# A hybrid decoder layer on one core: larger rings for keys and values, attention outputs kept in DRAM, and another order in the merged stage

## What is computed

```python
def _layer(x, S0, past_k, past_v, ...):
    xn = _rms(x, norm1_w)
    zq, zk, zv, hq, hf, hi, hg = _split_proj(xn, w_in)
    q, k, v = _da_qkv(zq, zk, zv, qn_w, kn_w)
    if past_k is None:
        o_da = _da_prompt(q, k, v, lam)          # causal, 1024 tokens
    else:
        o_da = _da_decode(q, k, v, past_k, past_v, lam)   # 2048 cached + 8 new
    o_da = (_rms(o_da, subln_w) * (1.0 - lam_init)).reshape(B, T, DA_WIDTH)
    o_hg, S_new = _hgrn2(hq, hf, hi, hg, lb, S0, hg_norm_w)   # recurrent heads
    h = x + jnp.einsum("btc,cd->btd", jnp.concatenate([o_da, o_hg], axis=-1), w_out)
    y = h + _hier_moe(_rms(h, norm2_w), ...)     # 16 experts, top 1 group, top 2 inside
```

## Time and profile before

| what | us |
|---|---|
| median of 3 runs | 1530.07 |
| lowest and highest of them | 1523.56, 1531.3 |
| the profiled execution | 1530.65 |
| its span, first to last instruction | 1528.9 |
| merged stage, from the barrier before it | 592.3 to 948.2 |
| experts, from about | 1134 |

### The profile page before, as it was taken

The page is one execution under the profiler, slowest core; times in us unless marked ns, Lnnn a source line. Parts: engine busy times, 40 slices in busy tenths (PEclk is TensorE's granted clock), DMA queues, the critical chain, the costliest instruction groups (busy, mean ns, idle before and its releaser), DMA issues. The chain is left out here.

```text
span 1528.9 us, 24713 instructions
## 1 busy us (share of the span) xinstructions
PE 1163.0 (76%) x9100; PEld 874.1 (57%) x9100; DVE 581.6 (38%) x1022; ACT 461.0 (30%) x857; POOL 239.3 (16%) x262
## 2 busy tenths in 40 slices
PE   4699998697979794167666757899839989999940
PEld 3699998486868683055444544677624434444410
DVE  5220110363636363466777773311252111121131
ACT  6111100444444454355555554212100100111121
POOL 4100000000000002121222221212011212222231
PEclk9999999698989897578787779899859999999975
DMA  4420310211111114778788774832133898887567
GB/s 120 110 63 22 84 29 25 74 44 57 57 57 57 57 44 129 231 238 268 245 260 265 244 248 146 302 136 97 62 109 96 230 286 262 253 261 204 128 140 185
DMA packets 160578, 226.50 MB, mean 148 GB/s; under 512 B 16081, under 2 KB 104402, under 8 KB 160402
## 3 DMA queue, kind: packets, MB, share of 16 engines
q1 hardware_dynamic: 133826, 168.63, 33.9%
q0 software_dynamic: 12992, 46.93, 12.3%
q10 hardware_dynamic: 13664, 9.64, 2.2%
HBM read 182.17 MB, written 47.45 MB: 150 GB/s over the span
## 5 line engine op out<-in xcount | busy, mean ns | idle before, releaser
L2135 PE MATMUL ps<-ring,e_xgT 128*128 x400 | 182.1, 609 | 8.7 <-SPq L2056 8.7
L2135 PEld LDWEIGHTS ps<-ring,e_xgT 128*128 128x128 f32 x400 | 76.2, 195 | 97.6 <-issue 97.6
L2164 PE MATMUL ps<-ring,e_hT 128*128 x200 | 92.4, 605 | 16.9 <-ACT e_hT L2193 16.9
L629 PE MATMUL ps<-xh,a_wh 128*128 128x384 f32 (+1 forms) x288 | 101.4, 352 | 0.0
L629 PE MATMUL ps<-xl,a_wh 128*128 128x384 f32 (+1 forms) x288 | 97.3, 338 | 0.0
L629 PE MATMUL ps<-xh,a_wl 128*128 128x384 f32 (+1 forms) x288 | 97.0, 337 | 0.0
L2087 POOL DMA_INDIRECT y_rows<-e_oE,slot_to x32 | 50.5, 1579 | 276.6 <-issue 224.8
L2188 ACT ACTIVATE e_sg<-ps 128x256 f32<-128x256 f32 x32 | 12.3, 383 | 256.2 <-PE ps L2135 243.6
L1559 DVE STREAM_TRANSPOSE d_KT<-d_K 128x2048 f32<-128x2048 f32 x32 | 73.7, 2304 | 23.3 <-DMA d_K<-in_cache_k 23.2
L1087 POOL TENSOR_TENSOR h_X<-h_X,h_q 128x256 f32<-128x256 f32 (+1 forms) x56 | 45.9, 830 | 232.6 <-ACT h_X L1344 117.2
L501 DVE COPY p_vs<-ps 128x256 f32<-128x256 f32 (+1 forms) x36 | 15.3, 424 | 173.5 <-PE ps L449 173.5
(11 more groups left out here) (342 smaller groups left out, 2476.2 us busy)
## 6 DMA issues: line engine op xcount, KB each, us to landing
d_K<-in_cache_k SPq DMA_DIRECT2D x128, 256.0 KB, 3.7
d_V<-in_cache_v SPq DMA_DIRECT2D x128, 256.0 KB, 3.8
ring<-in_w_gate SPq DMA_DIRECT2D x16, 1024.0 KB, 7.8
ring<-in_w_up SPq DMA_DIRECT2D x16, 1024.0 KB, 12.0
ring<-in_w_down SPq DMA_DIRECT2D x16, 1024.0 KB, 13.8
zT<-a_zs POOLq DMA_DIRECT2D x12, 544.0 KB, 3.0
a_w<-in_w_in SPq DMA_DIRECT2D x12, 512.0 KB, 3.8
y_rows<-ring SPq DMA_DIRECT2D x10, 512.0 KB, 2.6
```

The costliest lines, as they stand in the source:

```text
L629: ins = pe.matmul(m.ps[:, 7, 0:w0], left[:, n % 2, k, :], right[:, k, c0:c0 + w0], start=(k == 0 and j == 0), stop=(k == KD - 1 and j == 2))
L2135: ins = pe.matmul(m.ps[:, 2 + u, :], xgT[:, u, k, :], up_k[:, bass.ds(r * KD + k, 1), :].squeeze(1), start=(k == 0), stop=(k == KD - 1))
L2164: ins = pe.matmul(m.ps[:, 6 + b, :], hT[:, u, f * 128:f * 128 + 128], down_w[:, bass.ds(r * FC + f, 1), b * 512:b * 512 + 512].squeeze(1), ...
```

## The change

- **Keys and values.** KR goes from 2 to 3 and VR from 3 to 4, so that the ring of values holds a whole sequence. `load_values` takes the page numbers that `load_keys` read for the same group, and reads none itself.
- **Attention outputs.** `mixT` is split. `mixA` [128, 4, 1088] holds the attention half only until the prompt attention ends; GpSimd stores it, head by head, to a DRAM tensor `mix_rows`, and waits at the end of that block for all four stores. `mixH` is the recurrent half, `mixS` the attention output of the 64 new tokens. Mix loads `mix_rows` back in two DMAs (512 KB and 1.5 MB) on ScalarE's queue, and `split_mix` rounds and subtracts each half by its own instruction: four per tile instead of two.
- **VectorE.** `maximum` comes right after `picked_out`, ahead of `cumulate`, `with_keys` and `subs` 1. `subs` 5 and 6 of a unit are done at the start of that unit, after `collect`, and no longer at the end of the one before.
- **ScalarE.** `maps` comes ahead of `decays`, `load_next` and `norm`. `level_exps` 5 and 6 of a unit stand after `turned_keys`, ahead of `gates` of the next.
- **TensorE.** `output` comes after two groups of `values`, not three.

```diff
@@ -113,19 +113,22 @@
-        m.mixT = sb("mixT", [128, KD, TOK])
+        m.mixH = sb("mixH", [128, HEADS, TOK])
+        m.mixS = sb("mixS", [128, HEADS, NS])
+        m.mix_rows = nc.dram_tensor("mix_rows", (HEADS, 128, SEQ), F32, kind="Internal").ap()
         m.hn_rows = nc.dram_tensor("hn_rows", (TOK, D), F32, kind="Internal").ap()
...
-        m.z_stored, m.v_stored = (ctx.enter_context(nc.semaphore(n)) for n in ("z_stored", "v_stored"))
+        m.z_stored, m.v_stored, m.mix_stored = (ctx.enter_context(nc.semaphore(n)) for n in ("z_stored", "v_stored", "mix_stored"))
         with ExitStack() as middle:
...
                 m.xh = early.enter_context(nc.sbuf_tensor("xh", [128, KD, TOK], F32R))
+                m.mixA = early.enter_context(nc.sbuf_tensor("mixA", [128, HEADS, TOK], F32))
                 m.halves = early.enter_context(nc.sbuf_tensor("halves", [128, 128], F32))
@@ -468,7 +471,7 @@
                 for g, (c0, w0) in enumerate(GROUPS):
-                    dst = m.mixT[:, bass.ds(t + HEADS * n, 1), c0:c0 + w0].squeeze(1)
+                    dst = (m.mixA, m.mixH)[n][:, bass.ds(t, 1), c0:c0 + w0].squeeze(1)
                     ins = act.activation(dst, m.ps[:, 3 * n + g, 0:w0], ACT.Copy)
@@ -593,6 +596,9 @@
                     pool.sem_inc(z_left, 1)
+                pool.wait_ge(head_done, h + 1 + 1)
+                pool.dma_start(m.mix_rows[h, :, :], m.mixA[:, h, 0:SEQ]).then_inc(m.mix_stored, 16)
+            pool.wait_ge(m.mix_stored, HEADS * 16)
@@ -683,7 +689,7 @@
                 for n, s in enumerate((sq, sk)):
-                    z = m.mixT[:, bass.ds(h + HEADS * n, 1), :].squeeze(1)
+                    z = (m.mixA, m.mixH)[n][:, bass.ds(h, 1), :].squeeze(1)
                     act.activation(s[:, :], z, ACT.Square).then_inc(squared[n], 1)
@@ -759,7 +765,7 @@
             def prepare(h):
-                zq, zk = (m.mixT[:, bass.ds(h + HEADS * n, 1), :].squeeze(1) for n in range(2))
+                zq, zk = (mix[:, bass.ds(h, 1), :].squeeze(1) for mix in (m.mixA, m.mixH))
                 dve.wait_ge(r_ready[0], h + 1)
@@ -806,7 +812,7 @@
                 dve.wait_ge(ro_ready, h + 1)
-                dve.scalar_tensor_tensor(m.mixT[:, h, 0:SEQ], oT[:, :], m.subw[:, :], ro[:, :],
+                dve.scalar_tensor_tensor(m.mixA[:, h, 0:SEQ], oT[:, :], m.subw[:, :], ro[:, :],
                                          ALU.mult, ALU.mult).then_inc(head_done, 1)
@@ -832,7 +838,7 @@
     KEYS = PAGES * PAGE
-    KR, VR = 2, 3
+    KR, VR = 3, 4
     assert UNITS == DB
@@ -947,7 +953,7 @@
         def gate_of(n):
-            return m.mixT[:, n // 2 + HEADS, n % 2 * W:n % 2 * W + wide(n)]
+            return m.mixH[:, n // 2, n % 2 * W:n % 2 * W + wide(n)]
@@ -987,6 +993,8 @@
+            pages_of = {}
+
             def page_numbers(g):
@@ -994,14 +1002,14 @@
             def load_keys(g):
-                pages = page_numbers(g)
+                pages = pages_of[g] = page_numbers(g)
                 if g >= KR:
...
             def load_values(g):
-                pages = page_numbers(g)
+                pages = pages_of.pop(g)
                 if g >= VR:
@@ -1271,9 +1279,10 @@
                     sample_states(n)
-                for g in range(3):
-                    values(n, g)
+                values(n, 0)
+                values(n, 1)
                 output(n)
+                values(n, 2)
                 values(n, 3)
@@ -1426,19 +1435,21 @@
             logs(0)
             decays(0)
             load_next(1)
-            level_exps(0, 1, LEVELS)
+            level_exps(0, 1, 5)
             for n in range(UNITS):
                 more = n + 1 < UNITS
                 turned_keys(n)
+                level_exps(n, 5, LEVELS)
                 if more:
                     gates(n + 1)
                     logs(n + 1)
+                maps(n)
+                if more:
                     decays(n + 1)
                     if n + 2 < UNITS:
                         load_next(n + 2)
                 if n:
                     norm(n - 1)
-                maps(n)
                 if more:
                     level_exps(n + 1, 1, 2)
                 new_map_out(n)
@@ -1448,7 +1459,7 @@
                 if more:
-                    level_exps(n + 1, 2, LEVELS)
+                    level_exps(n + 1, 2, 5)
                 squares(n)
@@ -1619,43 +1630,45 @@
                 more = n + 1 < UNITS
                 if n:
                     collect(n - 1)
+                    subs(n, 5)
+                    subs(n, 6)
                 for i in range(3):
                     take(n, i)
                 if more:
                     queries(n + 1)
                 if n:
                     picked_out(n - 1)
+                maximum(n)
                 if more:
                     cumulate(n + 1)
                     with_keys(n + 1)
-                    subs(n + 1, 1)
-                maximum(n)
                 for i in range(3, 6):
                     take(n, i)
+                if more:
+                    subs(n + 1, 1)
                 states(n)
                 if more:
                     keys(n + 1, 0)
                 sums(n)
+                if more:
+                    subs(n + 1, 2)
                 if n:
                     finish(n - 1)
                 if more:
-                    subs(n + 1, 2)
                     keys(n + 1, 1)
                     subs(n + 1, 3)
                 if n % 2:
                     sample_states(n)
                 if more:
+                    keys(n + 1, 2)
                     subs(n + 1, 4)
-                    keys(n + 1, 2)
-                    subs(n + 1, 5)
-                    subs(n + 1, 6)
                     keys(n + 1, 3)
             collect(UNITS - 1)
             picked_out(UNITS - 1)
             finish(UNITS - 1)
             dve.wait_ge(d_ready, 1)
             ro = P[:, HEADS * NS:2 * HEADS * NS].rearrange("p (h t) -> p h t", h=HEADS)
-            dve.scalar_tensor_tensor(m.mixT[:, 0:HEADS, SEQ:TOK], m.kS[:, :, :], m.subw[:, :], ro, ALU.mult, ALU.mult)
+            dve.scalar_tensor_tensor(m.mixS[:, :, :], m.kS[:, :, :], m.subw[:, :], ro, ALU.mult, ALU.mult)
 def mix_phase(nc, a, m):
@@ -1705,6 +1718,7 @@
         gate = sem("m_gate")
+        mixA, mix_in = sb("m_mixA", [128, HEADS, SEQ]), [sem("m_mix_in0"), sem("m_mix_in1")]
         w_rounded, w_split, mix_rounded, mix_split = (sem(f"m_{n}") for n in (
@@ -1776,9 +1790,15 @@
                     pool.sem_inc(gate, 1)
-                pool.tensor_copy(mh[:, u, :, 0:n], m.mixT[:, :, cols(t)]).then_inc(mix_rounded, 1)
-                pool.wait_ge(mix_rounded, t + 1)
-                pool.tensor_tensor(ml[:, u, :, 0:n], m.mixT[:, :, cols(t)], mh[:, u, :, 0:n], ALU.subtract).then_inc(mix_split, 1)
+                o, g = mixA[:, :, cols(t)] if t < NT else m.mixS[:, :, :], m.mixH[:, :, cols(t)]
+                ho, hg = mh[:, u, 0:HEADS, 0:n], mh[:, u, HEADS:KD, 0:n]
+                pool.tensor_copy(hg, g).then_inc(mix_rounded, 1)
+                if t in (0, 2):
+                    pool.wait_ge(mix_in[t // 2], 16)
+                pool.tensor_copy(ho, o).then_inc(mix_rounded, 1)
+                pool.wait_ge(mix_rounded, 2 * t + 2)
+                pool.tensor_tensor(ml[:, u, HEADS:KD, 0:n], g, hg, ALU.subtract).then_inc(mix_split, 1)
+                pool.tensor_tensor(ml[:, u, 0:HEADS, 0:n], o, ho, ALU.subtract).then_inc(mix_split, 1)
             split_mix(0)
@@ -1812,7 +1832,7 @@
                     if b == 0:
-                        pe.wait_ge(mix_split, t + 1)
+                        pe.wait_ge(mix_split, 2 * t + 2)
                     if t >= 2:
@@ -1869,6 +1889,8 @@
         def _(act):
+            for i, c in enumerate((slice(0, 256), slice(256, SEQ))):
+                act.dma_start(mixA[:, :, c], m.mix_rows[:, :, c].rearrange("h p n -> p h n")).then_inc(mix_in[i], 16)
             load_ln_exp(nc, act)
```

## The result

The changed kernel takes 1516.98 us (median of four runs, 1514.59 to 1520.32), the kernel before 1529.25 (1523.56 to 1531.3): a ratio of 0.992, with a 95% interval of 0.9893 to 0.9947. It is faster, by 12 us. I had forecast 1504 in a range of 1485 to 1523: the sign and the range hold, the size doesn't. Less than half of the 26 us that I counted came. So the traces show some 16 us between the kernels where the medians show 12.

What follows compares the result with a forecast made beforehand. A chain of waits, not a full engine, was taken to set the merged stage's pace. Terms 3.6 - 16.4 - 18.6 + 0 + 4.5 = -26.9 against 1530.65 gave 1503.7, said as 1504; range 1485 to 1523.

Steps and rivals of the forecast that it cites:

- the term of the odd units: Merged stage, units 1, 3 and 5: 36.5 us each from the last key transpose to TensorE's end of the unit.
- D to D: Between ends of the last key transpose for units 1 and 7: six units, three pairs of 73.5, 220.5 us.
- C: Rival: transfers are the bound, pairs stay at 79.7 us, total 1522, or 1525 with mix's upper end; chance 0.09.
- D: Rival, slower: the last key group is late in every unit of the merged stage, 1539 and above; chance 0.07.
- E: Rival: the wait for values stays, their last group still late; pairs gain 4, total 1518; chance 0.03.
- Edge of the attention, +3.6: End of the prompt attention: GpSimd's last store and its wait add 3.6 us; ends 3.0 and 5.
- Unit 0, -16.4: First unit of the merged stage: key groups sent earlier save 16.4 us; ends -15 and -19.5.
- Even units, 37.0: Merged stage, units 2, 4 and 6: 37.0 us from TensorE's start, ScalarE held 4.0 by its DMA issues.
- rival A: More hidden than counted: even units 4.0 shorter, odd ones 1 shorter, 15 less in all, 1489; chance 0.20.
- Unit 7: Last unit of the merged stage, 33.3 us before: change 0, with 2 to 3 us each way.
- Start of mix: Mix reads 2 MB more: +4.5 us, ends 1 and 7; 6.9 if all of it delays the output weights.
- B: Rival: half of the pairs' gain, keys late and `norm` dearer; pairs give 9, mix 7, total 1516; chance 0.16.

Runs made afterwards that it cites:

- the fastest kernel: The changed kernel with sample states early, DMA issues on GpSimd, norm and squares first, and TensorE's order undone: 1476.91 us, 0.9635 of before.

## Why the prediction was right, and where it was wrong

The forecast gain was 26 us and 12 came. The step that failed is the term of the odd units, 36.5 us each: they took 39.9, 42.9 and 38.3, which is 11.6 of the 13.8 us by which the six units missed (220.5 counted, 234.3 measured from D to D). Two prices in it were too low, the new score and what follows the sample states.

**What bounds the kernel**: right. The waits for values are gone, in the middle they were replaced by waits on the engines' own order, and transfers are no bound in the six units: rivals C, D and E did not come. Two of my signs did not come either: the pairs took 77.5, 78.9 and 78.9 us, not 72 to 75, and the merged stage ended at 930.5, not by 917. The windows even reach a share of 0.96 in the fastest kernel with hardly a wait for keys.

**Edge of the attention, +3.6**: +5.1 from VectorE's last product to the first load (0.3 before), just over my upper end of 5. The store goes out 0.7 us after the product and lands, by the page's median for the four of them, 2.9 after its issue; another 1.8 pass from there to the first load. For the 0.7 and the 1.8 together I had taken 0.6. The attention itself ended 1.9 us earlier in this execution, so the account shows +3.2.

**Unit 0, -16.4**: -16.2, but by two errors that cancel. The four key groups were turned at 625.88, 30.3 us into the stage (counted 30.7), right. Unit 1's keys were ready at D = 658.35, 62.8 us into the stage, 4.3 us earlier than the 67.1 I counted. And I set my 659.4, an end of keys, against 675.8, TensorE's start of the unit, where before's end of keys was 671.3: 4.5 us too much. Two marks of the same unit are not one.

**Odd units, 36.5 each**: this is the step that failed. Measured from D to the end of TensorE's unit: 39.9, 42.9 and 38.3, together 11.6 us over. Of these, 6.4 lie before the end of the sample states, which came at D+33.5, D+31.0 and D+30.6 (counted D+29.6), and 5.2 behind it.

The first part goes with the new score. I priced it at 4.57, the fastest of the three odd units before, whose others took 6.38 and 4.92 (at 679.21 and 839.41). After the change it took 7.07, 6.85 and 6.25 us from its first product to its last, 6.5 over. The 7.07 ran at a mean granted clock of 0.58, behind a stop of 3.25 us; the other two ran at 0.97 and 1.00 and have idle time of 1.3 and 1.0 within them. What lengthened them is not shown.

```profile
664.00 7.07 PE L1225 MATMUL ps<-d_KT,d_q 32*32 32x512 f32 x128
```

What follows the sample states was sized by rows at a clock of 1.00, but for the last: output 4.1, two groups 2.0, new values 0.65, together 6.8. In unit 1 it took 6.4 at a clock of 1.00, in unit 3 11.8, nearly all at 0.50, and in unit 5 7.7 at 0.81. I had written that "TensorE's `output` waits for that" and priced the wait, not the clocks that were measured behind it, and not that a ready group stood behind it. (The terms of the odd unit add up to 36.4, not 36.5.)

**Even units, 37.0**: 36.6, 36.0 and 40.5. Two were right within a microsecond, unit 4 step by step: queries were done at 10.7 us (counted 9.8), `states` at 22.9 (23.2), the end came at 36.0. In unit 6 ScalarE was held 10.3 us by its issues and not 4.0, and everything after moved by as much, less the slack. I had kept the row of unit 2, the longest of the three before (4.0, 1.2 and 2.6), with rival A on the side of less. The other side, issues that get longer, was not among my cases. That `norm` gives back a part was right, with 28.1 us of waits before `state_steps`.

**Unit 7**: from D of unit 7 to the end of the stage +0.9, within the 2 to 3 each way. **Start of mix**: the first product came 8.8 us after the stage's first load, within the 8 to 10, 3.0 later than before. But at the end of mix only 1.3 of it is left, so the 6.9 us of bytes were nearly all covered, and my 4.5 was too high. **Experts**: unchanged (+0.5).

**The rivals**: B, at 1516, is the number that came, by luck: its pairs gained 9 and its mix cost 7, where the trace has 5.6 and 1.3. Its first reason, keys that land late, was wrong: VectorE waits 0.8 us for keys in the six units. Its second, a dearer `norm`, did not come in unit 4, where `norm` ended at 20.2 us as counted. The 353 GB/s of C's dense stretch is not the most that the core moves: from 854.77 to 862.36 the changed kernel moved 381. The range's lower end was added up wrongly: A with the lowest unit 0 and mix is 1482, not 1485.

## What to carry to other kernels

When a transfer's wait is removed, price what is then last at each TensorE clock that the traces show (the same products took 6.2, 7.6 and 11.6 us here, at 1.00, 0.81 and 0.50, behind waits of 3 to 5 us), and take a term from all its rows, not from the fastest. Look whether ready work stands behind the waiting instruction: one group of products put back ahead of it was worth 9.9 us by the medians. Thirteen DMA issues at a unit's end held ScalarE for up to 12.8 us beside a busy SyncE; moving them to an engine off the path brought 8.6 us, and the engine that took them made another wait. Of several edits that come together, measure each alone: here one part (the rings) brought 30 us, one cost 7 and one 9.5.
